# Half of the last tile's residual by an adding transfer: new order at the first pair and at the end of a two-layer diffusion step

## What is computed

```python
def trunk_layer(l, x, cond, ...):
    mod = jax.nn.silu(cond) @ w_ada[l] + b_ada[l]
    shift, scale, gate = jnp.split(mod[:, None, :], 3, axis=-1)
    h = rmsnorm(x, norm_pre[l]) * (1 + scale) + shift
    proj = h @ w_in[l]
    ...
    x = x + gate * rmsnorm(o @ w_out[l], norm_post[l])
    return x, k, v
```

## Time and profile before

| | |
|---|---|
| median of 3 runs | 1109.66 us (1109.39 to 1110.69) |
| the profiled execution | 1109.84 us |
| its span, first to last instruction | 1108.0 us |
| mean granted TensorE clock | 0.996 |
| busy: TensorE matmuls | 1079.7 us (97%) |
| busy: VectorE | 756.6 us (68%) |
| busy: ScalarE | 462.9 us (42%) |
| busy: POOL | 55.1 us (5%) |

### The profile page before, as it was taken

One profiled execution on the slowest core, in us unless ns is written; L12 is line 12 of the kernel. 1 busy time (PEld: TensorE's weight loads), 2 busy tenths in 40 slices (PEclk: granted clock), 3 DMA queues, 4 the chain that ended last, 5 costly groups with the idle time before them and its releaser, 6 DMA issues.

```text
span 1108.0 us, 13716 instructions
## 1 busy us (share of the span) xinstructions
PE 1079.7 (97%) x5308; PEld 867.4 (78%) x5308; DVE 756.6 (68%) x1092; ACT 462.9 (42%) x745; POOL 55.1 (5%) x91
## 2 busy tenths in 40 slices
PE   6999999999999999999999999999999999999995
PEld 4576687887878878788887788888888888887884
DVE  4555565766677786699956745487756766389777
ACT  4333334433636342243346842323343322275553
POOL 1000010000000000000010000000000000002120
PEclk9999999999999999999999999999999999999998
DMA  9998866454545577667884244445544655577966
GB/s 379 416 401 335 335 243 251 167 228 159 221 187 212 212 279 297 237 229 291 309 329 175 76 152 163 161 171 190 175 171 187 228 193 187 170 163 146 305 149 170
DMA packets 42208, 250.68 MB, mean 226 GB/s; under 512 B 5104, under 2 KB 5216, under 8 KB 16800
## 3 DMA queue, kind: packets, MB, share of 16 engines
q1 hardware_dynamic: 28656, 186.66, 43.8%
q0 software_dynamic: 10800, 58.88, 17.7%
q10 hardware_dynamic: 2688, 4.26, 1.3%
HBM read 246.06 MB, written 3.72 MB: 225 GB/s over the span
## 4 chain that ended last, share of the span: by engine, by line
PE 87%; DMA 5%; DVE 5%; ACT 2%; issue 1%; POOL 0%; DVEq 0%; ACTq 0%; SPq 0%
PE bank L1267 23%; PE bank L1269 22%; PE bank L1268 22%; DMA raw_first<-in_ada_first 3%; PE bank L1330 2%; PE bank L1215 2%; PE bank L1216 2%; PE bank L1217 2%; PE bank L1412 2%; DMA raw<-in_w_out 1%; PE bank L1351 1%; DVE w_lo L1877 1%; PE bank L1476 1%; PE bank L1428 1%; PE bank L1391 1%
## 5 line engine op out<-in xcount | busy, mean ns | idle before, releaser
L1267 PE MATMUL bank<-w_hi,h_op 128*128 128x512 f32 x1036 | 419.4, 405 | 2.1 <-DVE h_op L2124 1.6
L1269 PE MATMUL bank<-w_hi,h_op 128*128 128x512 f32 x1036 | 405.1, 391 | 0.0
L1268 PE MATMUL bank<-w_lo,h_op 128*128 128x512 f32 x1036 | 404.1, 390 | 0.0
L1877 DVE TENSOR_TENSOR w_lo<-raw,w_hi 128x1024 fp32r<-128x1024 f32 x210 | 256.3, 1222 | 146.3 <-ACT w_hi L1526 145.9
L1526 ACT ACTIVATE w_hi<-raw 128x1024 fp32r<-128x1024 f32 x210 | 220.4, 1056 | 199.4 <-PE bank L1269 162.5
L1267 PEld LDWEIGHTS bank<-w_hi,h_op 128*128 128x128 f32 x1036 | 194.7, 188 | 54.3 <-issue 16.4
L1269 PEld LDWEIGHTS bank<-w_hi,h_op 128*128 128x128 f32 x1036 | 194.5, 188 | 42.0
L1268 PEld LDWEIGHTS bank<-w_lo,h_op 128*128 128x128 f32 x1036 | 195.0, 188 | 36.8
L1881 DVE SCALAR_TENSOR_TENSOR dot_raw<-dot_raw,cond_sb 128x2048 f32<-128x2048 f32 x32 | 72.9, 2279 | 0.0
L1709 ACT ACTIVATE probs_t<-bank 128x384 f32<-128x384 f32 (+1 forms) x36 | 15.2, 421 | 83.0 <-PE bank L1435 83.0
L1881 DVE SCALAR_TENSOR_TENSOR late_junk<-raw,cond_half 128x1024 bf16<-128x1024 f32 x32 | 39.0, 1220 | 1.3 <-DMA cond_half<-cond_rows 1.3
(11 more groups left out here) (298 smaller groups left out, 1291.0 us busy)
## 6 DMA issues: line engine op xcount, KB each, us to landing
raw<-in_w_in SPq DMA_DIRECT2D x68, 1024.0 KB, 5.2
dot_raw<-in_ada_tiles POOLq DMA_DIRECT2D x32, 1024.0 KB, 5.1
raw<-in_w_out SPq DMA_DIRECT2D x28, 1024.0 KB, 6.6
raw_first<-in_ada_first SPq DMA_DIRECT2D x21, 1024.0 KB, 12.6
raw<-in_ada_groups SPq DMA_DIRECT2D x16, 1024.0 KB, 6.7
raw<-in_ada_halves SPq DMA_DIRECT2D x16, 1024.0 KB, 4.8
open_raw<-in_w_in SPq DMA_DIRECT2D x24, 512.0 KB, 12.9
raw<-in_w_out POOLq DMA_DIRECT2D x24, 512.0 KB, 8.0
```

Source lines behind the costliest of these rows:

```text
L1267: pe.matmul(out, operand(layer, kind, 0, k, t), hi, start=k == begin, stop=False)
L1268: pe.matmul(out, operand(layer, kind, 0, k, t), lo, start=False, stop=False)
L1269: last = pe.matmul(out, operand(layer, kind, 1, k, t), hi, start=False, stop=k == end)
L1877: dve.tensor_tensor(lo, src, hi.bitcast(F32), ALU.subtract).then_inc(lo_ready, 1)
```

## The change

Three things are changed.

1. **The order at the start of each pair.** In pair 0, G's sum is made at step 13 instead of 10 and E's at 15 instead of 11; E, H5 and G are rounded at steps 17, 19 and 25 instead of 13, 15 and 22, and split two steps after. Pair 0's first join, its first two squares and its first two takes move from steps 27, 22, 31, 26 and 34 to 34, 28, 37, 32 and 40, and the fourth gate row of both pairs from 29 to 35.
2. **A stored base.** After the last load of w_in, SyncE stores x as layer 0 left it for those columns of the outputs to which something is added later: all of tile 1, the first half of tile 2, three quarters of tile 0.
3. **The end.** For these columns ScalarE scales `mixed` (five entries "scale_half", of 1024 columns, the last of 512) and POOL's queue adds it onto the stored base by transfers into HBM (`accum_op=ALU.add`). VectorE adds to x only the pieces (0, 3), (2, 2) and (2, 3), which SyncE stores. POOL's own sum of a piece is gone.

```diff
+SCALED = [(1, 0, D // 2), (1, D // 2, D), (0, 0, D // 2), (2, 0, D // 2), (0, D // 2, 3 * D // 4)]
+END_ORDER = [(0, 3), (2, 2), (2, 3)]
...
-    for i, entry in ((9, "H1"), (10, "G"), (11, "E")):
+    for i, entry in ((9, "H1"), (13, "G"), (15, "E")):
         put(FIRST_PAIR, i, "combine", entry)
-    for i, entry in ((11, "H1"), (13, "E"), (15, "H5"), (22, "G"), (34, "H3")):
+    for i, entry in ((11, "H1"), (17, "E"), (19, "H5"), (25, "G"), (34, "H3")):
         put(FIRST_PAIR, i, "round_combined", entry)
         put(FIRST_PAIR, i + 2, "split_combined", entry)
...
-    for i, j in ((47, 0), (48, 1), (50, 2), (50, 3)):
-        put(c, i, "piece_end", 1, j)
+    put(c, 48, "scale_half", 0)
+    put(c, 50, "scale_half", 1)
...
+            sp.wait_ge(x_ready, len(X_ORDER))
+            sp.dma_start(y_sample[0, 0:P, :], x[:, 1, :]).then_inc(base_stored, 16)
+            sp.dma_start(y_sample[0, P:2 * P, 0:D // 2], x[:, 2, 0:D // 2]).then_inc(base_stored, 16)
+            sp.dma_start(y_prompt[0][:, 0:3 * D // 4], x[:, 0, 0:3 * D // 4]).then_inc(base_stored, 16)
...
-            pool.wait_ge(piece_scaled, 1)
-            pool.tensor_tensor(x[:, 0, cols], x[:, 0, cols], mixed[:, 0, cols], ALU.add).then_inc(piece_added, 1)
+            pool.wait_ge(base_stored, 16 * 3)
+            for n, (t, begin, end) in enumerate(SCALED):
+                pool.wait_ge(half_scaled, n + 1)
+                dst = y_prompt[0] if t == 0 else y_sample[0, (t - 1) * P:t * P, :]
+                pool.dma_start(dst[:, begin:end], mixed[:, t, begin:end], accum_op=ALU.add).then_inc(grown_y, 16)
...
+                elif what == "scale_half":
+                    t, begin, end = SCALED[e[1]]
+                    act.wait_ge(inverted, PAIR_END.index(t) + 1)
+                    act.activation(mixed[:, t, begin:end], mixed[:, t, begin:end], ACT.Copy, scale=stat[:, 3, t:t + 1])\
+                        .then_inc(half_scaled, 1)
```

More of the change, by code:

```diff
@@ L412, in timetable @@
             put(c, i, "pair_gate", p, n)
-        put(c, 29, "pair_gate", p, 3)
+        put(c, 35, "pair_gate", p, 3)
         for i, n in ((9, KEEP_P1), (40, KEEP_U2), (50, KEEP_P7)):
@@ L416, in timetable @@
         if p < LAST_PAIR:
-            joins = (27, 1), (42, "rest"), (44, 2), (57, 4), (61, 5)
-            squares = (22, 0), (31, 1), (47, 2), (52, 3), (60, 4), (64, 5)
-            takes = (26, 0), (34, 1), (50, 2), (56, 3), (63, 4), (67, 5)
+            joins = (34, 1), (42, "rest"), (44, 2), (57, 4), (61, 5)
+            squares = (28, 0), (37, 1), (47, 2), (52, 3), (60, 4), (64, 5)
+            takes = (32, 0), (40, 1), (50, 2), (56, 3), (63, 4), (67, 5)
         else:
@@ L432, in timetable @@
     put(c, 47, "invert_end", 1)
-    for i, j in ((47, 0), (48, 1), (50, 2), (50, 3)):
-        put(c, i, "piece_end", 1, j)
+    put(c, 48, "scale_half", 0)
+    put(c, 50, "scale_half", 1)
     put(c, 52, "y_end", 0)
     put(c, 54, "invert_end", 0)
-    put(c, 54, "piece_end", 0, 0)
-    put(c, 55, "piece_end", 0, 1)
-    put(c, 55, "scale_piece", 0, 3)
-    pre(len(CHUNKS), "y_sum", 2)
+    put(c, 54, "scale_half", 2)
+    put(c, 55, "y_sum", 2)
     pre(len(CHUNKS), "join", p, 5)
     pre(len(CHUNKS), "square", p, 5)
-    pre(len(CHUNKS), "piece_end", 0, 2)
+    pre(len(CHUNKS), "piece_end", 0, 3)
     pre(len(CHUNKS), "take", p, 5)
@@ L446, in timetable @@
     pre(len(CHUNKS), "invert_end", 2)
-    for j in range(PIECES):
+    pre(len(CHUNKS), "scale_half", 3)
+    pre(len(CHUNKS), "scale_half", 4)
+    for j in (2, 3):
         pre(len(CHUNKS), "piece_end", 2, j)
@@ L781, in hybrid_step @@
         x_ready = sem("x_ready")
-        piece_scaled = sem("piece_scaled")
-        piece_added = sem("piece_added")
+        inverted = sem("inverted")
+        half_scaled = sem("half_scaled")
+        base_stored = sem("base_stored")
+        grown_y = sem("grown_y")
         x_squared = sem("x_squared")
@@ L1028, in _ @@
                         sp.dma_start(raw[:, slot, :], w[:, k * CW:(k + 4) * CW]).then_inc(raw_in[slot], 16)
-            def store_piece(t, j):
+            for n, (t, j) in enumerate(END_ORDER):
+                sp.wait_ge(x_ready, len(X_ORDER) + n + 1)
                 dst = y_prompt[0] if t == 0 else y_sample[0, (t - 1) * P:t * P, :]
@@ L1033, in store_piece @@
                 sp.dma_start(dst[:, cols], x[:, t, cols]).then_inc(stored, 16)
-            for n, (t, j) in enumerate(END_ORDER):
-                sp.wait_ge(x_ready, len(X_ORDER) + n + 1)
-                store_piece(t, j)
-                if (t, j) == (2, 0):
-                    sp.wait_ge(piece_added, 1)
-                    store_piece(0, 3)
-            sp.wait_ge(stored, 16 * TOKS * PIECES)
+            sp.wait_ge(stored, 16 * len(END_ORDER))
+            sp.wait_ge(grown_y, 16 * len(SCALED))
             sp.wait_ge(k_stored, 16)
@@ L1905, in add_piece, with invert_y @@
                                          in1=x[:, t, cols], op0=ALU.mult, op1=ALU.add).then_inc(x_ready, 1)
-            def invert_y(layer, t):
-                if layer:
-                    wait_acc(dve, PAIRS[-1][t < 2], t)
-                else:
-                    wait_acc(dve, LAST[0], t)
-                dve.wait_ge(y_root, TOKS + PAIR_END.index(t) + 1 if layer else PLACE[t] + 1)
+            def invert_y(t):
+                wait_acc(dve, LAST[0], t)
+                dve.wait_ge(y_root, PLACE[t] + 1)
                 then_own(dve.reciprocal(stat[:, 3, t:t + 1], stat[:, 2, t:t + 1]))
             def residual_end(t):
-                invert_y(0, t)
+                invert_y(t)
                 dve.wait_ge(x_again, 16 * TOKS)
@@ L2385, in part @@
                 elif what == "invert_end":
-                    invert_y(1, e[1])
+                    t = e[1]
+                    wait_acc(dve, PAIRS[-1][t < 2], t)
+                    dve.wait_ge(y_root, TOKS + PAIR_END.index(t) + 1)
+                    dve.reciprocal(stat[:, 3, t:t + 1], stat[:, 2, t:t + 1]).then_inc(inverted, 1)
+                elif what == "piece_end":
+                    dve.wait_ge(inverted, PAIR_END.index(e[1]) + 1)
                     dve.wait_ge(x_ready, len(X_ORDER))
-                elif what == "piece_end":
                     add_piece(*e[1:])
```

8 lines of the change are left out of this document (removed).

## The result

The changed kernel took 1117.34 us (median of 4 executions, 1116.63 to 1117.94) against 1109.64 us (4 executions, 1109.39 to 1110.69) for the kernel before on the same chip: a ratio of 1.0068, 95% interval 1.0053 to 1.0083. It is 7.7 us **slower** (0.7%), where no difference was forecast, and above the range (1108.0 to 1114.2). The profiled execution took 1117.1 us with a span of 1115.3; before, 1109.84 and 1108.0. So 7.3 us of span have to be found.

What follows compares the result with a forecast made beforehand. The number of TensorE matmuls was taken to bound the kernel, then an uncovered end of 11.8 us. +1.65 (pair 0's start) - 0.3 (end) = +1.35 on 1109.84 gave 1111.2, against the median 1111.0 us; range 1108.0 to 1114.2.

Steps and rivals of the forecast that it cites:

- Part 1, the gap: Start of pair 0: new order delays TensorE behind t1 by a gap of 3.1 us; TensorE's end moves +1.65 us.
- two idle places of VectorE: Start of pair 0: VectorE waits for ScalarE's roundings before halves 8 and 11 of the weights, 1.02 us idle each.
- half 12: Pair 0's weights, numbered by use: b22's first half, forecast to start on TensorE at 1004.35, 1.9 us later than before.
- the late wait ahead of pair 1: At 1035.87 TensorE waits 0.25 us for a half whose transfer landed late; forecast to go.
- The clock: Rival, 12%: granted clock falls in the gap before half 12, losing 1.7 to 3.4 us: 1112.7 to 1114.4.
- the forecast: Whole kernel: the main case, 1111.0 us, no difference that can be told; given 58%.
- Part 2, the base stores: After the last w_in load: three transfers of x take the engines 5.6 us and cost nothing.
- Part 3 up to the inversion: The end: VectorE joins at 1096.69 and inverts at 1098.94 instead of 1100.79, 1.85 us won.
- Part 3, the transfers: The end: last adding transfers land at 1105.7 and 1107.3, against 1107.6 before: -0.3 us.
- my 200 GB/s: Rate taken for queued adding transfers from earlier ones into SBUF: 1.60 MB in 8 us, 2.6 us per 512 KB.
- upper bound, +4.0: The end: worst earlier adding transfer, 11.2 us to land, would put the last landing at 1111.6.
- adding into HBM is slower than into SBUF: Rival, 8%, at the end: at double, 5.2 us per 512 KB, the kernel takes 1113 to 1120.

Runs made afterwards that it cites:

- after_again: The changed kernel measured once more, unaltered: 1116.5 us (5 executions) against 1109.96 for the kernel before, 1.0058.
- order_pair2: order_only measured once more, side by side with a kernel with filling matmuls: 1113.6 us, 7 of 11 executions at 1113.0 or more.
- order_only: The kernel before with only the new order of work at the pairs' start: 1111.91 us against 1109.78, 1.0023.
- tail_only: The changed kernel with the old order at the pairs' start, so base stores and new end alone: 1112.93 us, 1.0030.
- tail_plain: tail_only with plain transfers in place of the adding ones, leaving out that sum: 1108.76 us against 1109.78, 0.9992.

## Why the prediction was wrong

- **Part 1, the gap: right.** The two idle places of VectorE were predicted at 1.02 us each and measured 0.94; half 12 was predicted at 1004.35 and came at 1004.35 (to the hundredth by luck: H5's splits started 0.11 us sooner than predicted, and the matmul came 0.11 us later behind them); the late wait ahead of pair 1 went, as said. Without the clock's fall the last matmul came 1.4 us later (after_again), predicted 1.65.
- **The clock: a rival at 12% where it is the usual case.** What it does was right (it falls at this gap, and costs 1.6 us in the changed kernel's trace and 2.7 in order_pair2's, for a price of 1.7 to 3.4), the chance was not. The step said that it decides "from a gap about as long as mine", and then took the forecast as if it did not. Of four traces with this gap three show the fall, and of order_only's 18 executions ten lie at 1113 or more. The Trainium skill, "TensorE: Matmul & The Clock Gate", section "Part 1: The HAM clock gate", says that the chip's watch on TensorE's activity runs freely and does not start with the kernel; the trace agrees in that the same gap brings the clock down in one execution and not in the next, and the fall comes 1.5 us after work has resumed (the changed kernel), 0.5 us after it (order_only) or before its first matmul (order_pair2).
- **Part 2, the base stores: right.** They landed 8.3 to 12.0 us behind their issue and made the next two w_out loads land after 7.6 and 9.7 us instead of 4.8 and 7.1; tail_only's last matmul, 0.36 us earlier than before's, shows no cost.
- **Part 3 up to the inversion: right.** 1.9 us won, 1.85 predicted; a scaling of 1024 columns 1.16 us, 1.2 taken.
- **Part 3, the transfers: the step that failed.** "The first lands at 1105.7", "may push it by 0 to 0.5; I take 1107.3". I gave the queue to the last two transfers alone and half a microsecond to all that lay ahead. POOL's requests came when predicted (4.4 and 5.0 us behind the last matmul, predicted 4.2 and 5.05), but the two landed 7.8 and 8.9 us after them. The engines' work has to be added up from where they are full: from the adding transfer at 1100.67 on, 1.31 MB of adding at my 200 GB/s are 6.5 us and 0.79 MB of plain stores at 420 GB/s 1.9 us. That is an estimate of 8.4 us behind a first latency of 2.7 (5.3 less 2.6), so 1111.8 in the new trace; it was 1113.19. The rest lies where the engines do not end together: they are full until 1111.0 (share 1.07) and then at 0.27 and 0.10 for two more microseconds. Predicted was 11.1 us behind the last matmul, measured 13.9 and, in the two other traces of this tail, 13.05 (after_again) and 13.2 (tail_only). So the term was -0.3 and measured +2.5; the step's own upper bound, +4.0, took this in. The rival "adding into HBM is slower than into SBUF" does not hold: the first one, alone, landed after 5.3 us, as the quickest of the earlier trace rows. Nor does the fit of the Trainium skill ("DMA: Bandwidth & Descriptors", section "Anatomy of one DMA — SWDGE (gpsimd) path") for adding transfers: it gives an estimate of 3.2 us for 512 KB, and they took 5.3. Plain ones on this queue, in tail_plain, took 2.9, near the fit.
- **What no step held: the closing DRAIN.** I priced POOL's queue up to its landing and took the 0.4 us behind it from before. It was 2.1.

The sum as measured is 1.9 + 1.6 - 0.35 + 2.5 + 1.7 = 7.35 (7.3 by the spans), where +1.35 was forecast. The difference is 2.8 by the transfers, 1.7 by the closing DRAIN and 1.6 by the clock. Two of these terms were in the text and undersized, one was missing; any one of them alone would have stayed inside the range. Part by part the medians of the two halves (order_only +2.1 and +3.7 in its two measurements, tail_only +3.15) make 5.3 to 6.8, and the whole was 6.5 and 7.7.

## What to carry to other kernels

Behind the last transfer of a program count the issuing engine's own end, and keep the last transfers off POOL's queue: here it costs 1.5 us in the trace and 1.6 by the median for a single plain one, and 1.7 with the adding ones. Where several transfers go out within one latency, add up the engines' work from the first on; two adding ones that end early were worth having (1.6 us, together with POOL's sum moved under the join), five at the end were not. A gap of 2.2 or 3.4 us between TensorE's matmuls costs more than itself in a part of the executions; where it can't be removed, unread matmuls in it keep the clock. A single trace does not show how often the clock falls: look at the spread of the executions, and at several traces before a detail of one of them is taken for an effect, as the gate row shows.
